# Projection weights loaded two units at a time, decay rows in long pieces, eight cache copies issued earlier

## What is computed

```
proj = u @ w_in                                # 1024 x 9248, float32
z, xbc, dt_raw, q, k, v, gate_a, gate_b = split(proj)
xbc_c = silu(causal_dwconv(xbc_ext, conv_w, conv_b))        # -> xs, Bm, Cm
y, h_new = ssd_scan(xs, dt, A, Bm, Cm, h0)     # two chunks of 128 for the prompt,
                                               # one recurrence step for each of 8 samples
branch_a = group_rms_norm(y * silu(z), g) @ w_out_ssm
branch_b = dilated window attention (three groups of heads) @ w_out_attn
x1 = layer_norm(ALPHA * x + (sigmoid(gate_a)*branch_a + sigmoid(gate_b)*branch_b) @ w_out)
x2 = layer_norm(ALPHA * x1 + top-4-of-32 mixture of experts (x1))
new caches = the old key/value caches of the samples, moved by one row, + the new row
```

## Time and profile before

| | |
|---|---|
| median of 3 runs | 1370.95 us (1370.46 to 1373.19) |
| profiled execution, own time | 1370.5 us |
| its span | 1368.8 us |
| mean granted TensorE clock | 0.992 |
| PE busy | 1308.8 us, 96% of the span |
| DMA moved | 539.93 MB, mean 394 GB/s |

### The profile page before, as it was taken

The page is one execution under the profiler, slowest core; times in us unless marked ns, Lnnn a source line. Parts: engine busy times, 40 slices in busy tenths (PEclk is TensorE's granted clock), DMA queues, the critical chain, the costliest instruction groups (busy, mean ns, idle before and its releaser), DMA issues.

```text
span 1368.8 us, 24720 instructions
## 1 busy us (share of the span) xinstructions
PE 1308.8 (96%) x10213; PEld 653.0 (48%) x10213; DVE 574.5 (42%) x896; ACT 296.7 (22%) x603; POOL 169.9 (12%) x232
## 2 busy tenths in 40 slices
PE   9998999999999999999999999999999999999996
PEld 7998899976765333333333333333333322333322
DVE  4988999878457322132223221112222122222114
ACT  6778665643211100000000000000000000000002
POOL 1006774404000000000000000000000000000000
PEclk9999999999999999999999999999999999999998
DMA  8998998999999999999999999999999999999994
GB/s 269 338 386 258 359 364 294 380 345 383 400 375 369 396 424 428 425 427 427 429 426 427 428 427 429 424 428 424 428 427 428 428 427 427 426 429 425 431 424 189
DMA packets 113637, 539.93 MB, mean 394 GB/s; under 512 B 12901, under 2 KB 76501, under 8 KB 80773
## 3 DMA queue, kind: packets, MB, share of 16 engines
q1 hardware_dynamic: 103866, 524.91, 94.8%
q10 hardware_dynamic: 8448, 9.83, 2.2%
q0 software_dynamic: 1264, 4.35, 0.8%
HBM read 522.69 MB, written 60.56 MB: 426 GB/s over the span
## 4 chain that ended last, share of the span: by engine, by line
PE 64%; DMA 26%; DVE 6%; issue 2%; ACT 1%; POOL 1%; SPq 0%; ACTq 0%; DVEq 0%; POOLq 0%
PE psum L2394 21%; DMA wnat<-in_w_down_dram 10%; PE psum L2417 10%; DMA wmx<-in_w_down_dram 8%; DMA whm<-in_w_down_dram 6%; PE psum L2380 5%; PE psum L1904 4%; PE psum L1905 4%; PE psum L1906 4%; PE psum L2106 3%; PE psum L2440 3%; PE psum L2444 2%; PE psum L2243 1%; DMA x_scratch<-xbc 1%; PE psum L2425 1%
## 5 line engine op out<-in xcount | busy, mean ns | idle before, releaser
L1779 DVE STREAM_TRANSPOSE hturn<-psum 128x1024 f32<-128x1024 f32 x32 | 40.0, 1250 | 402.6 <-PE psum L2394 402.6
L1904 PE MATMUL psum<-xh,wh 128*128 128x264 f32 x592 | 173.1, 292 | 3.8 <-ACT zz L829 3.2
L1906 PE MATMUL psum<-xh,wlow 128*128 128x264 f32 x592 | 168.5, 285 | 0.0
L1905 PE MATMUL psum<-xl,wh 128*128 128x264 f32 x592 | 168.3, 284 | 0.0
L1116 ACT ACTIVATE sg<-hb 128x512 f32<-128x512 f32 x32 | 20.2, 631 | 523.5 <-DVE hb L1788 523.5
L2394 PE MATMUL psum<-wmh,xst 128*32 128x512 f32 x1056 | 118.6, 593 | 0.9 <-DVE xst L1745 0.8
L762 POOL COPY gcol<-gm 128x3 f32 (+1 forms) x32 | 17.4, 543 | 811.0 <-DVE hb L1783 810.3
L1904 PEld LDWEIGHTS psum<-xh,wh 128*128 128x128 f32 x592 | 112.3, 190 | 10.7 <-ACT zz L829 4.8
L1905 PEld LDWEIGHTS psum<-xl,wh 128*128 128x128 f32 x592 | 112.4, 190 | 1.4 <-issue 1.4
L1906 PEld LDWEIGHTS psum<-xh,wlow 128*128 128x128 f32 x592 | 111.7, 189 | 0.0
L2417 PE MATMUL psum<-wnat,hst 128*64 128x512 f32 x400 | 91.6, 598 | 14.3 <-DMA wnat<-in_w_down_dram 10.9
(11 more groups left out here) (459 smaller groups left out, 1733.2 us busy)
## 6 DMA issues: line engine op xcount, KB each, us to landing
wmh<-in_w_gate_up_dram SPq DMA_DIRECT2D x33, 2048.0 KB, 34.8
spare<-in_w_gate_up_dram SPq DMA_DIRECT2D x21, 2048.0 KB, 30.5
wnat<-in_w_gate_up_dram SPq DMA_DIRECT2D x20, 2048.0 KB, 36.9
wnat<-in_w_down_dram SPq DMA_DIRECT2D x20, 2048.0 KB, 34.8
wraw<-in_w_in_dram SPq DMA_DIRECT2D x37, 1024.0 KB, 9.9
out_dram<-in_cache_kv_w_dram SPq DMA_DIRECT2D x32, 1023.5 KB, 11.7
whm<-in_w_gate_up_dram SPq DMA_DIRECT2D x12, 2048.0 KB, 35.6
wmx<-in_w_gate_up_dram SPq DMA_DIRECT2D x11, 2048.0 KB, 37.5
```

What stands on the lines that cost most here:

```text
L1779: v.transpose(hturn[:, :].rearrange("p (f c i) -> p f c i", c=4, i=QW), psum[:, at:at + 2, :].rearrange("p h (f i c) -> p (h f) c i", c=4, ...
L1904: mm(out, hi[:, k, :], xh[:, k, :], start=(k == 0), stop=False)
L1905: mm(out, hi[:, k, :], xl[:, k, :], start=False, stop=False)
L1906: last = mm(out, lo[:, k, :], xh[:, k, :], start=False, stop=(k == KT - 1))
```

## The change

1. Projection units are loaded in pairs: where two units from u = 2 to 31 lie in neighbouring places of the ring (places 0 and 1, or 2 and 3), one transfer of 2 MB brings both, with rows of 2 KB in place of 1 KB. The units in place 4, units 0 and 1, and those from 32 on are loaded singly. The pair is loaded at the turn of its first unit, and waits until both places are free: for the tiles of unit u-4 and not only of u-5. Where the place that comes free was itself part of a pair, the wait is for the end of that pair.
2. The decay rows lie in DRAM by group and chunk, so that `acb` is read in rows of 4 KB in place of eight rows of 512 bytes. ACT writes them with four transfers in place of one.
3. Eight copies are issued in the projection, at the odd u from 19 to 33, and no longer behind the loads of w_out_ssm (five pieces behind the first five, three behind the next three). So copies stand at every u from 18 on.

```diff
+        def load_of(u):
+            return u - u % RING % 2 if 2 <= u < 32 and u % RING < 4 else u
+        def units_of(u):
+            return 2 if load_of(u + 1) == u else 1
+        def raw_ready(eng, u):
+            n = load_of(u)
+            loads = sum(load_of(v) == v for v in range(n % RING, n + 1, RING))
+            eng.wait_ge(S(f"raw_landed{n % RING}"), 16 * loads)
...
-                src = a_scratch[gi * HPG:(gi + 1) * HPG, c * P:(c + 1) * P].unsqueeze(0).broadcast_to([P, HPG, P])
-                sp.dma_start(acb[:, it % 3, :, :], src).then_inc(S(f"acb_in{it % 3}"), 16)
+                src = a_scratch[gi, c].rearrange("h l -> (h l)").unsqueeze(0).broadcast_to([P, HPG * P])
+                sp.dma_start(acb[:, it % 3, :, :].rearrange("p h l -> p (h l)"), src).then_inc(S(f"acb_in{it % 3}"), 16)
...
                 if u >= RING:
-                    sp.wait_ge(S("tile_done"), 2 * (u - RING) + 2)
-                    if 5 < u < 17 or u > 33 or (u >= 18 and u % 2 == 0):
+                    before = u + units_of(u) - 1 - RING
+                    sp.wait_ge(S("tile_done"), 2 * (load_of(before) + units_of(load_of(before)) - 1) + 2)
+                    if 5 < u < 17 or u > 17:
                         move_cache(next(pieces))
-                load(u, wraw[:, u % RING, :].rearrange("p (k n) -> p k n", k=KT), w_in_v[:, :, w_in_col(u):w_in_col(u) + 256])
+                if load_of(u) == u:
+                    load(u, raw_place(wraw, u), w_in_v[:, :, w_in_col(u):w_in_col(u) + 256 * units_of(u)])
...
             for i in range(RING):
                 native(i)
-                for _ in range(3):
+                for _ in range(2):
                     move_cache(next(pieces))
...
                 native(i)
                 move_cache(next(pieces))
-                if i < N_SSM:
-                    move_cache(next(pieces))
...
-                    act.dma_start(a_scratch, acum[:, :, :].rearrange("h c l -> h (c l)")).then_inc(S("a_out"), 16)
+                    for gi in range(GROUPS):
+                        act.dma_start(a_scratch[gi].rearrange("c h l -> h c l"), acum[gi * HPG:(gi + 1) * HPG, :, :]).then_inc(
+                            S("a_out"), 16)
```

More of the change, by code:

```diff
@@ L322, in build, with raw_place @@
         wdn = w_down[0]
-        def raw_ready(eng, n):
-            eng.wait_ge(S(f"raw_landed{n % RING}"), 16 * (n // RING + 1))
+        def load_of(u):
[6 more added lines that the diff above has]
+            eng.wait_ge(S(f"raw_landed{n % RING}"), 16 * loads)
+        def raw_place(ring, u):
+            first, n = load_of(u), units_of(load_of(u))
+            at = ring[:, first % RING:first % RING + n, :].rearrange("p a w -> p (a w)")
+            return at.rearrange("p (k n) -> p k n", k=KT)
         def native_slot(i):
@@ L335, in half_of @@
         def half_of(ring, m):
-            return ring[:, (m // 2) % RING, :].rearrange("p (k n) -> p k n", k=KT)[:, :, (m % 2) * P:(m % 2) * P + P]
+            u = m // 2
+            at = (u - load_of(u)) * 256 + (m % 2) * P
+            return raw_place(ring, u)[:, :, at:at + P]
         def high_of(m):
@@ L352, in conv_tile @@
             return 16 + f if f < X0 else f - X0
-        a_scratch = nc.dram_tensor("a_scratch", (HEADS, TP), F32, kind="Internal").ap()
+        a_scratch = nc.dram_tensor("a_scratch", (GROUPS, 2, HPG, P), F32, kind="Internal").ap()
         x_scratch = nc.dram_tensor("x_scratch", (ZT, P, TS), F32, kind="Internal").ap()
@@ L478, in _ @@
                 if u >= RING:
-                    sp.wait_ge(S("tile_done"), 2 * (u - RING) + 2)
-                    if 5 < u < 17 or u > 33 or (u >= 18 and u % 2 == 0):
+                    before = u + units_of(u) - 1 - RING
+                    sp.wait_ge(S("tile_done"), 2 * (load_of(before) + units_of(load_of(before)) - 1) + 2)
+                    if 5 < u < 17 or u > 17:
                         move_cache(next(pieces))
-                load(u, wraw[:, u % RING, :].rearrange("p (k n) -> p k n", k=KT), w_in_v[:, :, w_in_col(u):w_in_col(u) + 256])
+                if load_of(u) == u:
+                    load(u, raw_place(wraw, u), w_in_v[:, :, w_in_col(u):w_in_col(u) + 256 * units_of(u)])
                 if u == 9:
-                    sp.wait_ge(S("a_out"), 16)
+                    sp.wait_ge(S("a_out"), 16 * GROUPS)
                 if u in (9, 11, 13):
@@ L591, in _ @@
                 if m == 4:
-                    for piece in pieces:
-                        move_cache(piece)
                     sp.wait_ge(S("native_used"), N_SSM)
```

## The result

The changed kernel takes 1389.68 us (median of 4 runs, 1386.68 to 1394.66), the kernel before 1370.70 us beside it (4 runs). The ratio is 1.0138, with a 95% interval of 1.0106 to 1.0170: 19 us slower. The direction and the range of the prediction hold, and the point is 4.7 us too low. The span of the profiled execution is 1388.3 us, 19.5 more than the 1368.8 of before.

The account below looks back on a forecast made before the run. The compute chain up to the expert stream's start was taken to bound the kernel. Delays of 4.5 (`x_scratch`), 3.5 (states), 5 (`y_scratch`) and 1 (clock) sum to 14 us over 1370.5, forecast 1385 us, range 1374 to 1394.

Parts of the forecast that it names:

- A microsecond that the compute chain loses before 386 us is lost at the end: Before the first expert load at 386.25 us: compute delays reach the end in full.
- What counts is when it starts: End of the kernel: the expert stream at 427 GB/s can't be hurried, so its start sets the end.
- to the use of xdts: Near 100 us: `x_scratch`, behind the pair (17, 18) and its wait for tile 28, makes `xdts` late, +4.5 us.
- clock: PE, after new stalls: spells at the lower clock, one to three times, add +1 us.
- The signs: Expected in the changed trace: later `x_scratch`, DVE waits for a state and `ysf`, first expert load at about 399 us.
- none of it on the chain except at the two waits: Projection: 10 to 20 us of queue time saved, but only 1.49 and 0.96 us of waits near 100 us can gain.
- delays the same DVE work by less and is covered by this: ACT's wait for unit 15, up to 4 us later in its pair, adds nothing beyond `x_scratch`'s +4.5 us.
- States, +3.5: Near 165 us: `state_in(3)`, behind the pair (22, 23) and a copy, lands late for DVE, +3.5 us.
- y_scratch and ysf, +5: Near 237 to 252 us: copies and units 32 and 33 ahead of `y_scratch` make `ysf` late, +5 us.
- overfull: Queue from 110 to 237 us: the added copies exceed its room by about 8 us, so it is never empty.
- The saving of the longer rows: Whole projection: pairs and longer `acb` rows save 10 to 20 us of queue time.
- Rival D: Whole kernel held by its transfers: saved queue time starts the expert stream earlier, 1355 to 1367 us; chance 0.09.

Follow-up runs that it names:

- pairs and decays: The kernel before with paired loads and decay rows in long pieces, the eight copies not moved: 1388.12 us, ratio 1.0121.
- early expert loads: One or two expert loads issued ahead of the last w_out load, on the kernel before with long decay rows: 1368.65 us with one, 1374.27 with two.
- x first: The changed kernel with `x_scratch`, its wait and the read of `xdts` issued ahead of the wait for the pair of units 17 and 18: 1388.90 us.
- copies alone: The kernel before with only the eight copies moved, single loads and short decay rows kept: 1375.85 us, ratio 1.0044.
- pairs alone: The kernel before with only the projection's loads paired, decay rows and copies kept; also spelled pairs only: 1386.85 us, ratio 1.0134.
- y clear: The changed kernel with the copies at units 32 and 33 issued right behind the read of `ysf`: 1391.22 us, ratio 1.0153.
- one pair (2, 3): The kernel before with units 2 and 3 alone loaded as one pair: 1378.81 us, ratio 1.0061.
- late waits, no pairs: The kernel before with single loads, where the first unit of each later pair waits one unit of compute more: 1381.61 us, ratio 1.0074.
- decays only: The kernel before with only the decay rows in long pieces: 1367.53 us, ratio 0.9982.

## Why the prediction was right, and where it was not

**What bounds the kernel.** "A microsecond that the compute chain loses before 386 us is lost at the end" held: span less first expert load was 982.6 us before, 982.0 to 983.2 in every kernel of the table but pairs and decays (986.4, with PE's wait of 2.9 us for w_out in it). "What counts is when it starts" was too strong, as the early expert loads show.

**By place.** DVE's use of `xdts`, `y_scratch` and the first expert load split the loss. `xdts` was used at 121.05 us in place of 112.03; from there on by the two SP rows:

| stretch | predicted | measured |
|---|---|---|
| to the use of xdts | 4.5 | 9.0 |
| from there to y_scratch | 3.5 | 7.8 |
| from y_scratch to the first expert load | 5 | 3.1 |
| clock | 1 | in the above |
| sum | 14 | 19.9 |

The signs moved the same way: `x_scratch` landed at 119.16 us (I had 113 to 117), DVE waited for a state at 174.5 (165) and for `ysf` at 265.6 (252), and the first expert load is at 406.15 (399). The granted clock of 110 to 237 us was 0.97, before 0.99.

The range held and the direction too, but the sum is closer than its terms: two of them are half of what was measured, and the third is larger. That the point came out within 5 us is in part luck.

**To the use of xdts: a cost that the prediction put at nothing.** It said that savings are "none of it on the chain except at the two waits" and gave no cost to the pairs ahead of (15, 16). But a pair is there only when both its units are. In the changed kernel PE waited for ACT behind the landing of the pair (2, 3), and again near 90 us, behind a pair that took 12.64 us to land:

```profile
32.68 0.39 PE L1922 MATMUL psum<-xh,wh 128*128 128x264 f32 x1 [2.04 <-ACT ctmp L842]
...
90.59 0.39 PE L1922 MATMUL psum<-xh,wh 128*128 128x264 f32 x1 [0.60 <-ACT ctmp L842]
```

Tile 6 ended at 38.75 us in place of 36.20, and tile 28 at 106.94 in place of 103.51: 3.4 us late. `x_scratch` was issued right behind that tile, at 107.39 where I had 104, and that is these 3.4 us. SP was not held by its queue there: it stood 8.0 us in the wait for tile 28, and the issue of `x_scratch` took 0.58 us, where it took 4.51 before. So the queue that stood idle from 24 to 60 us does not show in the time of `x_scratch` in this kernel; PE's delay does. I had let the transfer land 1.3 us faster after its issue than before, since less would be ahead of it; it landed after 11.77 us, for 11.93. That makes up the 9.0: 5.8 for the later wait, 3.4 for PE, and 0.2 less for the landing.

DVE's wait for `xdts` was 1.6 us where I had said 6, since DVE itself was late by ACT, which had unit 15 only at 109.4 us, 15.01 us after its issue. The prediction did say that the wait for unit 15 "delays the same DVE work by less and is covered by this": both came out about equally late. With x first, only the first was taken away, and nothing came back.

**States, +3.5, were mis-sized at 7.8.** I had the state behind a pair and a copy. It also stands behind its predecessor's store: SP's wait for stores rose from 19.3 to 44.4 us. With the copies alone it was 40.7 us, with the pairs alone 24.1. But both parts of the change make states late: from the issue of `x_scratch` to that of `y_scratch` the copies alone take 3.6 us more than before and the pairs alone 2.2, with 8.4 and 10.0 us of DVE's waits for states. DVE waited four times in the changed kernel, at 4.6 us the longest, where I had counted one state.

**y_scratch and ysf, +5, against 3.1.** They were late as I had said: 8.84 us to land and a wait of 4.4 us, where I had 3.2 with an empty queue. Whether this delay is what the stretch loses is not shown: without it (y clear) nothing came back.

**The rest.** The queue was not overfull from 110 to 237 us: its share was 0.89, for all the copies in it, with SP in waits for stores for 44.4 us of 120 to 260. The saving of the longer rows was about as sized, 9% in 60 to 90 us by GB/s over share (389 for 356, the last section has the table); over the 219 us from 18 to 237 that would be some 18 us, an estimate, near the upper end of my 10 to 20. Copies taken from the w_out_ssm loads gave nothing there, as predicted: from `y_scratch` to the first expert load it took 149.3 us before and 152.6 with the copies alone. Rival D, by which the saved queue time comes back as time, had the saving about right and not its effect: in the changed kernel the queue has more room (a share of 0.75 for 1.03 from 24 to 60 us), and the end comes 19 us later.

What stays open: how the 16.7 us of pairs divide between the wait (11.7, which holds the late unit 7 too) and the landing of two units at once. The landing has no run of its own over the whole projection. The one pair (2, 3) has both, and of its 8.2 us the part that is shown to come from the landing is PE's wait of 2.05 us. What of the changed kernel's loss behind 121 us is due to which wait isn't shown either: each that was taken away alone gave back nothing that the medians show.

## What to carry to other kernels

Before loads are joined, ask two things. When does the joined place come free? With 5 places and 2 units each, a pair is refilled a unit later, and that alone cost 11.7 us here. And who waits for its first half? It comes only with the second, and a delay of PE of 2 us near the start came back here in everything that is issued when a tile is finished. The rate that longer rows bring has to pay for both.

A share of 1.0 over a long stretch says that there is no slack in the queue, and not that the queue holds the end: look at the transfer that matters, and whether its issuer stood in a wait (the changed kernel, 8.0 us for tile 28) or in issues (the one pair, 5.09 us for `x_scratch`). Where several waits are as large as each other, a local repair moves the wait. The one part that gained here took queue time away (the decays' short pieces) and left the order as it was.

## What the runs showed of the hardware

The reads of `acb` in rows of 512 bytes were dearer than their size. The GB/s of 60 to 90 us over its share says what the queue moves while it is busy:

| kernel | GB/s | share | GB/s over share |
|---|---|---|---|
| before | 360 | 1.01 | 356 |
| late waits, no pairs | 387 | 1.09 | 355 |
| one pair (2, 3) | 383 | 1.06 | 361 |
| pairs only | 368 | 1.00 | 368 |
| decays only | 386 | 1.03 | 375 |
| pairs and decays | 370 | 0.96 | 385 |
| changed | 397 | 1.02 | 389 |

The two or three `acb` reads of that stretch (0.5 MB each), joined into long pieces, gain 5%; turning nearly all its loads of weights from rows of 1 KB into 2 KB gains 3%, with and without the long decays. The first three rows have the same row lengths but for one pair, and differ by 2%, so the 3% are little more than that scatter. I had taken 0.3 us for a read; 19 GB/s over 30 us are 1.6 us at 356 GB/s, 0.5 to 0.8 for each. The Trainium skill ("DMA: Bandwidth & Descriptors", Specifications) puts the smallest transfer for line rate at 512 bytes. The table disagrees: in this mix of loads, copies and states rows of 512 bytes still gained by being made longer, and those of 1 KB seem to.
